# Gathering an expert's tokens as quarter rows and turning them on VectorE, with the sample tokens routed inside the last output product

## What is computed

```
mix = concat([o_gla, o_swa], -1) @ w_out
x1 = layer_norm(DEEPNORM_ALPHA * x + mix, ln1_g, ln1_b)
logits = x1 @ w_router + b_router            # 32 experts
top_val, top_idx = lax.top_k(logits, 4)      # 4 experts for each token
gate_w = softmax(top_val)
# for each expert e, for its own tokens xe only:
h = clamped_swiglu(xe @ w_gate[e] + b_gate[e], xe @ w_up[e] + b_up[e])
y = (h @ w_down[e] + b_down[e]) * gate_w
out = layer_norm(DEEPNORM_ALPHA * x1 + sum of y, ln2_g, ln2_b)
```

## Time and profile before

| | |
|---|---|
| time, median of three runs | 1417.11 us (1416.81 to 1419.41) |
| the profiled execution's own time | 1416.46 us |
| its span in the profile | 1414.6 us, so 1.9 us lie around the span |
| TensorE busy (matmuls) | 1358.3 us, 96% |
| VectorE busy | 440.2 us, 31% |
| ScalarE busy | 299.1 us, 21% |
| GpSimd busy | 120.4 us, 9% |
| the queue of the weights, share of 16 DMA engines over the span | 75.6% |
| HBM read and written | 443.85 MB and 21.70 MB |

### The profile page before, as it was taken

The page is one execution under the profiler, slowest core; times in us unless marked ns, Lnnn a source line. Parts: engine busy times, 40 slices in busy tenths (PEclk is TensorE's granted clock), DMA queues, the critical chain, the costliest instruction groups (busy, mean ns, idle before and its releaser), DMA issues.

```text
span 1414.6 us, 43598 instructions
## 1 busy us (share of the span) xinstructions
PE 1358.3 (96%) x19522; PEld 872.2 (62%) x19522; DVE 440.2 (31%) x859; ACT 299.1 (21%) x637; POOL 120.4 (9%) x121
## 2 busy tenths in 40 slices
PE   7999999998999999999999999999999999999990
PEld 6767776555566666666666666666666666666660
DVE  3335656365322222222222222222222222222214
ACT  4544566131111111111111111111111111111104
POOL 1022000001010001000000100010000000100000
PEclk9999999998999999999999999999999999999995
DMA  8211042567999999999999999999999999999954
GB/s 276 60 50 46 16 145 74 210 234 280 413 405 397 405 401 405 397 403 403 406 403 403 403 403 396 403 401 407 397 404 401 408 401 401 401 399 389 405 216 135
DMA packets 78700, 459.80 MB, mean 325 GB/s; under 512 B 13344, under 2 KB 14896, under 8 KB 29232
## 3 DMA queue, kind: packets, MB, share of 16 engines
q1 hardware_dynamic: 67760, 429.74, 75.6%
q0 software_dynamic: 10256, 27.13, 7.2%
q10 hardware_dynamic: 512, 0.26, 0.1%
HBM read 443.85 MB, written 21.70 MB: 329 GB/s over the span
## 4 chain that ended last, share of the span: by engine, by line
PE 89%; DVE 6%; ACT 2%; issue 1%; DMA 1%; DVEq 0%; SPq 0%; ACTq 0%; POOLq 0%
PE unit L1274 47%; PE unit L1255 15%; PE unit L1258 9%; PE unit L1164 4%; PE unit L1243 3%; PE unit L763 2%; PE unit L765 2%; PE unit L764 2%; PE unit L758 1%; PE unit L891 1%; DVE attT L2185 1%; PE unit L915 1%; PE unit L798 1%; PE unit L1237 0%; ACT sbuf L1570 0%
## 5 line engine op out<-in xcount | busy, mean ns | idle before, releaser
L1274 PE MATMUL unit<-ring_b,xeT 128*32 128x256 f32 x6336 | 353.8, 381 | 1.1 <-ACT xeT L1420 1.1
L1274 PE MATMUL unit<-ring_a,xeT 128*32 128x256 f32 x5952 | 328.7, 379 | 0.0
L1274 PEld LDWEIGHTS unit<-ring_b,xeT 128*32 128x32 f32 x6336 | 203.7, 110 | 135.6 <-issue 2.7
L1274 PEld LDWEIGHTS unit<-ring_a,xeT 128*32 128x32 f32 x5952 | 192.6, 110 | 126.5
L1258 PE MATMUL unit<-ring_a,heT 128*32 128x256 f32 x768 | 169.7, 379 | 0.0
L1255 PE MATMUL unit<-ring_a,heT 128*32 128x512 f32 (+1 forms) x1536 | 169.4, 486 | 0.0
L1816 ACT ACTIVATE sg<-gm 128x768 f32<-128x768 f32 x32 | 27.0, 843 | 633.5 <-DVE gm L2456 633.5
L1258 PE MATMUL unit<-ring_b,heT 128*32 128x256 f32 x720 | 160.3, 379 | 0.0
L1255 PE MATMUL unit<-ring_b,heT 128*32 128x256 f32 (+1 forms) x1440 | 160.1, 486 | 0.0
L2484 DVE TENSOR_TENSOR hb<-unit,brow 128x768 f32<-128x768 f32 x32 | 30.7, 958 | 308.1 <-PE unit L1274 308.1
L700 POOL DMA_INDIRECT acc_rows<-ysb,idx x32 | 46.5, 1453 | 666.0 <-ACT ysb L1827 634.3
(11 more groups left out here) (318 smaller groups left out, 1264.8 us busy)
## 6 DMA issues: line engine op xcount, KB each, us to landing
ring_b<-w_gate_dram SPq DMA_DIRECT2D x68, 1024.0 KB
ring_a<-w_down_dram SPq DMA_DIRECT2D x68, 1024.0 KB
ring_b<-w_up_dram SPq DMA_DIRECT2D x64, 1024.0 KB
ring_a<-w_up_dram SPq DMA_DIRECT2D x64, 1024.0 KB
ring_a<-w_gate_dram SPq DMA_DIRECT2D x60, 1024.0 KB
ring_b<-w_down_dram SPq DMA_DIRECT2D x60, 1024.0 KB
raw_a<-w_in_dram SPq DMA_DIRECT2D x16, 512.0 KB, 3.7
wo<-w_out_dram SPq DMA_DIRECT2D x2, 1024.0 KB, 7.9
```

The lines of the kernel that those rows point to most:

```text
L1274: ins = mm(dst, stat(j), own[:, q], start=first and j != 1, stop=last and j != 0)
```

## The change

Five things change.

- **The table.** A row of `x1_rows` becomes four quarters of 288 floats: 256 features and a copy of the 32 gates each. GpSimd first copies a tile of `res` by quarters into `x1q` (a tensor copy of 128 x 1024), then stores 1 KB pieces; the gates are stored four times, in pieces of 128 bytes.
- **The gather.** Three indirect DMAs of 128 quarter rows (1152 bytes each) take the place of one of 96 whole rows. In gather j, partition 32q + l receives quarter q of slot 32j + l.
- **The row numbers.** `read_rows` also writes `spread`, the token list split by thirds; one more small matmul `to_quarters` and two small VectorE operations `quarter_rows` give `idxq`, which the gathers wait for. `rows_of` and its readers run one expert further ahead, in unit `px`.
- **The turn.** `x_T` and ScalarE's copy of `xeT` go. `x_turned` on VectorE transposes 128 x 256 in 32 x 32 blocks, three times for an expert, at the end of `dve_step`. ScalarE's `rows_in` keeps three small copies of the gate column.
- **The routing.** `x1_transposes(4)` and `logits(4)` are placed inside `out_product(3)`, behind its chunks 4 and 5. VectorE routes and gates tile 4 ahead of `first_norm(3)`. `ROUTED` is the new order: 0, 1, 4, 2, 3.

The code for tokens beyond the 96 slots is changed to match.

```diff
+            x1_quarters = x1_dram.rearrange("t (q f) -> (t q) f", q=4)
+            def gather():
+                for j in range(3):
+                    pool.indirect_dma_start(xq[:, j], None, x1_quarters,
+                                            bass.IndirectOffsetOnAxis(ap=idxq[:, j:j + 1], axis=0),
+                                            bounds_check=4 * T - 1, oob_is_err=False).then_inc(x_rows, 16)
...
+            def x1_by_quarter(n, i):
+                r = rows(i)
+                if n >= 2:
+                    pool.wait_ge(x1_out, 16 * n)
+                ps(nc.gpsimd.tensor_copy(x1q[n % 2][:r].rearrange("p (q c b) -> p c q b", q=4, c=4),
+                                         res[:r, i].rearrange("p (c q b) -> p c q b", c=4, q=4)))
+                ps.settle()
+                pool.dma_start(x1_dram[i * P:i * P + r].rearrange("t (q f) -> t q f", q=4)[:, :, 0:QUARTER],
+                               x1q[n % 2][:r].rearrange("p (q f) -> p q f", q=4)).then_inc(x1_out, 16)
...
-            for n, i in enumerate(TILES):
+            for n, i in enumerate(ROUTED):
                 pool.wait_ge(gates_ready, n + 1)
-                pool.dma_start(x1_dram[i * P:i * P + rows(i), D:XCOLS], gd[:rows(i), i]).then_inc(x1_out, 16)
+                r = rows(i)
+                pool.dma_start(x1_dram[i * P:i * P + r].rearrange("t (q f) -> t q f", q=4)[:, :, QUARTER:QCOLS],
+                               gd[:r, i].unsqueeze(1).to_broadcast([r, 4, NE])).then_inc(x1_out, 16)
             pool.wait_ge(x1_out, 16 * 2 * NT)
-            pool.wait_ge(idx_ready, 1)
-            gather(0)
+            pool.wait_ge(idxq_ready, 1)
+            gather()
...
             def pool_step(e, par, first=False):
                 if not isinstance(e, int) or e < NE - 2:
-                    pool.wait_ge(idx_ready, e + 3)
-                    pool.wait_ge(xT_done, e + 2)
+                    pool.wait_ge(idxq_ready, e + 3)
+                    pool.wait_ge(gcol_ready, e + 2)
                     pool.wait_ge(xe_ready, e + 2)
-                    pool.wait_ge(x_rows, (e + 2) * 16)
+                    pool.wait_ge(x_rows, (e + 2) * 48)
                     pool.sem_inc(turn_over, 1)
-                    gather(par + 2)
+                    gather()
...
+            def samples_routed(k):
+                if k == 4:
+                    x1_transposes(4)
+                if k == 5:
+                    logits(4)
+            out_product(3, samples_routed)
...
-            def x_T():
-                for k in range(KD):
-                    half = xg[:CAP, k // 2 * 256:(k // 2 + 1) * 256].rearrange("s (p k) -> s k p", k=2)[:, k % 2]
-                    ins = tr(px[:, k * P:k * P + CAP], half, ident[:CAP, :CAP])
-                ins.then_inc(xT_done, 1)
+            def to_quarters(n, out):
+                pe.wait_ge(idx_ready, n + 1)
+                mm(out, laneb[:CAP], spread[:CAP].rearrange("p j c -> p (j c)"), start=True, stop=True)\
+                    .then_inc(spread_done, 1)
...
             def pe_step(e, p2, m0):
                 no_more = e >= NE - 2
-                pe.wait_ge(x_rows, (e + 2) * 16)
-                pe.wait_ge(xe_ready, e + 1)
                 if e == 1:
                     pe.wait_ge(freed[3], USES[3] + 2)
-                x_T()
                 if not no_more:
-                    pe.wait_ge(picked, e + 3)
-                    pe.wait_ge(gate_read, e + 2)
-                    rows_of(tok_done, CAP)
+                    pe.wait_ge(idxq_ready, e + 2)
+                    to_quarters(e + 2, px[:, 0:9])
+                if e + 3 < NE:
+                    pe.wait_ge(picked, e + 4)
+                    pe.wait_ge(idx_ready, e + 3)
+                    rows_of(px, tok_done, CAP)
...
             def rows_in(n, par):
-                act.wait_ge(xT_done, n + 1)
...
+                act.wait_ge(x_rows, (n + 1) * 48)
+                for j in range(3):
...
+                    ins = copy(gcol[own, par:par + 1], src)
+                ins.then_inc(gcol_ready, 1)
...
             first_norm(4)
             route(1)
             gate(1)
+            route(4)
+            gate(4)
+            st(cp(row_part[:, 3:4], k_("slot")[:, 3:4]))
             first_norm(3)
             route(2)
-            route(4)
             gate(2)
-            st(cp(row_part[:, 3:4], k_("slot")[:, 3:4]))
             route(3)
-            gate(4)
             gate(3)
...
+            def x_turned(n, par):
+                v.wait_ge(x_rows, (n + 1) * 48)
+                v.sem_inc(turn_over, 1)
+                for j in range(3):
+                    src = xq[:, j, 0:QUARTER].rearrange("p (c a k) -> p c k a", c=4, k=2)
+                    ins = nc.vector.transpose(xeT[:, par, j], src)
+                ins.then_inc(xe_ready, 1)
...
             over_partitions(0, 0, gate_bias_in)
-            read_rows(1, 1)
+            read_rows(1, 1, pg)
             pick_rows(posm[:, :, 2:3], 2).then_inc(picked, 1)
+            x_turned(0, 0)
+            quarter_rows(1, pg[:, 1008:1017])
+            read_rows(2, 2, px)
+            pick_rows(posm[:, :, 3:4], 3).then_inc(picked, 1)
...
             def dve_step(e, par):
                 over_partitions(1, e, up_bias_in)
                 if not no_more:
-                    v.wait_ge(y_free, e + 1)
-                    read_rows(e + 2, (par + 2) % TURN)
...
+                    quarter_rows(e + 2, px[:, 0:9])
...
                 turned(heT_last if last else heT, e)
+                if not (isinstance(e, int) and e >= NE - 3):
+                    v.wait_ge(y_free, e + 2)
+                    read_rows(e + 3, (par + 3) % TURN, px)
...
                     gate_sig(e + 1)
+                if not no_more:
+                    x_turned(e + 2, par % 2)
```

More of the change, by code:

```diff
@@ L89 @@
 FOLD = 768
-QUARTER = D // 4
 def rows(i):
@@ L1169, in out_product @@
                                      start=k == 0, stop=k == KD - 1)
+                    if between is not None and k < KD - 1:
+                        between(k)
                 ins.then_inc(s_full(name), 1)
@@ L2469, in _ @@
             gate_sig(0)
+            x_turned(1, 1)
             def dve_step(e, par):
@@ L2592, in constants @@
     k("jcol")[:] = np.arange(MAXEXTRA)[None]
+    k("lane")[:] = p[:, None] % NS == p[None] % NS
+    k("third")[:] = np.repeat(p[:, None] // NS == np.arange(3)[None], 3, 1)
+    parts = np.stack([np.full(P, 4), np.full(P, 4), np.full(P, -4 * T), 4 * T + p // NS], -1)
+    k("quarter")[:] = np.tile(parts, (1, 3))
     s, t = p[:, None], p[None, :]
```

190 lines of the change are left out of this document (109 added, 81 removed).

## The result

The changed kernel took 1427.94 us (median of five runs, 1423.93 to 1432.47) beside 1417.56 for the kernel before (1416.81 to 1421.35, five runs): ratio 1.0064, 95% interval 1.0035 to 1.0093. It is slower, by some 10 us; 1407 and faster was forecast. The profiled execution took 1424.45 us with a span of 1422.6, 8.0 us more than before.

A forecast was written before the change was run, and what follows sets the result against it. TensorE bounds the experts, with the weights' DMA stream just as full and 10.0 us of lead left. Lead -10.0, start +3.0, gathers -2.2, routing 0 sum to -9.2 against 1416.46: 1407 us, range 1393 to 1430.

The forecast's parts named there:

- TensorE's step, -1.0 us x 31: Experts: each TensorE step loses x_T, 1.13 us, and gains a small matmul, 0.1; 31 us, of which 10.0 come through.
- The lead left, 10.0 us: End of the experts: last weights land 10.0 us before TensorE begins the last chunk, capping what a faster TensorE gains.
- The gathers' price to the stream, -0.07 for an expert: Expert weight stream: a gather costs 1.49 us of weights instead of 1.56; -2.2 us over 31 experts.
- the 0.80 excess: Weight stream during a gather: 0.80 us of the 1.56 us cost that the gather's own bytes don't explain.
- The first rival: Expert weight stream: gathers stop disturbing the weights, -0.47 us for an expert, -14.6 in all, 1395 us; chance 0.20.
- The start of the stream, +3.0: Before expert 0's w_down loads: longer row-number work, +0.85, and three gathers issued in turn, 2.1, delay the weights; +3.0 us.
- The routing, 0: Routing ahead of the experts: tile 4's earlier transposes, logits, route and gate cancel, between -1.7 and +1 us; taken as 0.
- The hold of `route(2)` by tile 3's copy: Routing: GpSimd's copy could block VectorE's route(2) through the shared port by up to 2.4 us, making 1409.
- VectorE, ScalarE and GpSimd in a step, nothing: Expert step: VectorE's added 1.4 us, ScalarE's copy dropped and the later gathers are covered; costed at nothing.
- small pieces dearer for the stream, 1430: Rival, expert weight stream: the excess grows with the pieces' time, a gather costs 2.24 us, +21 us, 1430; chance 0.21.
- The signs named ahead: Profile after: if right, small late chunk waits, steps 31.5 then 32.8 us, first gather landing near 336; if wrong, 31.5 throughout.

The follow-up runs named there:

- two chunks early: Kernel with the third gather held back from the second expert on, plus two of expert 0's four w_down loads issued before the gather lands: 1390.9 us, ratio 0.980.

## Why the prediction was wrong

- **TensorE's step, -1.0 us x 31.** Right: 0.98. It was counted as worth 10 us only, since the weights would bind.
- **The lead left, 10.0 us.** It was counted rightly for the kernel before, and the limit by the stream is real: with 96 partitions the steps grew longer from the nineteenth on.
- **The gathers' price to the stream, -0.07 for an expert.** Mis-sized: 0.62 less than before (32.78 to 32.16). Half of the 0.80 excess was taken to stay; in the changed kernel's window none does, as the weights lose 0.29 MB to 0.34. The first rival (-0.47, chance 0.20) named this mechanism, and the width as its cause. With 0.62 in the sum, 1416.46 - 10.0 + 3.0 - 19.2 = 1390: the complete kernels of three gathers over 128 partitions without pauses took 1391 to 1396.
- **The start of the stream, +3.0.** It was +4.7: `w_down` is issued at 337.73 instead of 333.04 (rows 11). From `posm` to the first gather's issue it is 0.88 longer (0.85 forecast), from that issue to the loads 2.38 longer (2.1 forecast). The other 1.4 us were there before the routing (tile 4's norm ended 1.55 us late, and 0.9 to 2.2 in the other kernels of the changed form whose clock held in the mixers); why, wasn't followed. The timeline after:

```profile
330.29 0.17 DVE L1962 TENSOR_REDUCE idxq<-row_parts 128x3 int32<-128x12 f32 x1
...
331.43 1.11 POOL L691 DMA_INDIRECT xg<-x_rows,idxq  x1 [3.52 <-DVE idxq L1962]
...
332.85 1.71 POOL L691 DMA_INDIRECT xg<-x_rows,idxq  x1 [0.30 <-issue]
...
334.86 1.00 POOL L691 DMA_INDIRECT xg<-x_rows,idxq  x1 [0.30 <-issue]
...
337.73 2.07 SPq L581 DMA_DIRECT2D ring_a<-w_down_dram  x4
...
339.26 2.36 PE L1318 MATMUL unit<-ring_b,xeT 128*32 128x256 f32 x20 [1.03 <-DVE xeT L2447]
```

- **The routing, 0.** Right, and GpSimd's copy of a tile took 1.04 us, within its bound of 2.4. The hold of `route(2)` by tile 3's copy, priced at 1409, didn't come: from the end of `first_norm(3)` to the `onehot` operation of `route(2)` it is 1.16 us with the copy (318.90 to 319.94) in between, and 1.15 before. **VectorE, ScalarE and GpSimd in a step, nothing.** As delays of the rows, right: the 20.86 us of a product are whole where there are no pauses, even with the third gather issued 15 us behind the first (912.28 to 927.41).
- **The step that failed** is the term put at nothing for GpSimd in a step. Its three issues were costed as a delay of the rows (2.4 us, covered) and of the stream, and TensorE's product was taken over unchanged at 20.86 us. That three gathers behind one another could slow TensorE in the middle of a product was no rival. The runs showed 21.98 - 20.74 = 1.24 us of pauses in each of some 30 steps, 37 us. The account of the span: start of TensorE +2.8 (336.46 to 339.26), steps -0.98 x 31 = -30, pauses +37, sum +9; measured +8.0. So the sum's main term, the 10.0 us by the lead, didn't apply: TensorE was never at the stream's limit. The time fell inside the range, near its upper end, by luck, for another reason than the rival there (small pieces dearer for the stream, 1430) gave.
- **The signs named ahead.** In the changed kernel none came: no waits for chunks, no steps of 31.5 us, the last chunk 30 us behind its weights, the first gather's landing near 337.7 instead of 336. In the kernels of three gathers without pauses the steps of 31.55 came, and the waits for chunks in the last steps (with 96 partitions from the nineteenth on); with two chunks early 31.55 held to the end, which was named as a sign of being wrong: the stream limits this form by 3 us, not by 21.

## What to carry to other kernels

A chain that shows one engine back to back gives the worth of work taken off it only if its own rate holds, so compare the time of one unchanged product first, before against after. Indirect gathers are better spread over all 128 partitions, and each issued when the one ahead of it has landed, where the rows have time: here that is worth 37 us in the steps on a chip that pauses. And a result that an edit seems to explain needs the unedited kernel beside it on the same chip.

## What the runs showed of the hardware

- Three indirect gathers over 128 partitions issued some 1.34 us apart made TensorE pause some 0.56 us at a time, mostly two to three times in a step, on three chips (and in the first measurement); two made about one pause on E, single ones none on F. On three other chips no kernel had any.
- A gather over 96 partitions cost the weights' stream 0.64 MB for its 0.31; three over 128 cost 0.29 for 0.34. Half of the DMA engines fell behind at either width (share 0.50, 207 GB/s near the end).
- TensorE idle for 4.9 us was followed by a granted clock of 0.57 over the next 5 us, and the wait cost 7.2 us.
- Ten semaphore increments of GpSimd, 0.08 us apart, placed between two gathers didn't delay the second: its issue began 1.43 us behind the other's.
